# Two orders at the head of the expert stage: the first expert's row splits and the third tile's sum

## The reference, cut to what matters

```python
def moe_ffn(x, ...):
    idx, w = route(xf, w_router, router_bias)          # 8 experts of 64 for each token
    y = routed_experts(...) + swiglu(xf, ws_gate, ws_up, ws_down)
# routed_experts, one block of up to 128 tokens at a time:
    y = swiglu(x_pad[tok], w_gate[e], w_up[e], w_down[e]) * wt[:, None]
    acc = acc.at[tok].add(y)
# and around it, in each layer:
    h = layer_norm(DN_ALPHA * h + ffn, ...)
def swiglu(x, wg, wu, wd):
    return (jax.nn.silu(x @ wg) * (x @ wu)) @ wd
```

## Time and profile before

| | us |
|---|---|
| median of three runs | 2134.94 |
| lowest and highest run | 2131.61 to 2135.66 |
| the profiled execution's own time | 2133.7 |
| its span, first to last instruction | 2131.9 |

### The profile page before, as it was taken

One profiled execution on the slowest core, in us unless ns is written; L12 is line 12 of the kernel. 1 busy time (PEld: TensorE's weight loads), 2 busy tenths in 40 slices (PEclk: granted clock), 3 DMA queues, 4 the chain that ended last, 5 costly groups with the idle time before them and its releaser, 6 DMA issues. The chain is left out here.

```text
span 2131.9 us, 33562 instructions
## 1 busy us (share of the span) xinstructions
PE 1988.9 (93%) x9013; PEld 1495.5 (70%) x9013; DVE 1489.1 (70%) x2484; ACT 1301.5 (61%) x2152; POOL 404.3 (19%) x309
## 2 busy tenths in 40 slices
PE   7998898999999999999978999999999999999994
PEld 6886697667777677777746556756767767777772
DVE  3766667568887788877746137567878778788884
ACT  3544473347787778777743224336777777787874
POOL 0000230012222222222213000001222222222221
PEclk9999999899999999999988999999999999999997
DMA  6320214359999999999974110437999999999994
GB/s 194 134 79 1 69 39 175 131 179 376 367 367 355 352 358 376 370 349 363 354 227 156 54 40 1 172 123 281 354 346 368 361 340 354 365 376 369 376 365 146
DMA packets 181033, 541.72 MB, mean 254 GB/s; under 512 B 26432, under 2 KB 57568, under 8 KB 180832
## 3 DMA queue, kind: packets, MB, share of 16 engines
q1 hardware_dynamic: 150688, 460.65, 57.9%
q0 software_dynamic: 25248, 69.25, 12.9%
q10 hardware_dynamic: 5024, 10.91, 1.3%
HBM read 506.75 MB, written 54.10 MB: 263 GB/s over the span
## 5 line engine op out<-in xcount | busy, mean ns | idle before, releaser
L1830 DVE TENSOR_TENSOR gu_l<-ring,gu_h 128x1024 fp32r<-128x1024 f32 x512 | 610.8, 1221 | 86.0 <-ACT gu_h L1694 75.8
L1694 ACT CAST gu_h<-ring 128x1024 fp32r<-128x1024 f32 x512 | 523.7, 1062 | 74.8 <-DMA ring<-in_moe_w_up 56.6
L1609 PE MATMUL bank<-gu_h,xgT_l 128*128 128x512 f32 x1024 | 416.0, 406 | 0.0
L1611 PE MATMUL bank<-gu_h,xgT_h 128*128 128x512 f32 x1024 | 403.4, 394 | 0.0
L1610 PE MATMUL bank<-gu_l,xgT_h 128*128 128x512 f32 x1024 | 402.0, 393 | 0.0
L1958 POOL DMA_INDIRECT xg<-h_rows,list_idx x128 | 149.6, 1169 | 902.0 <-issue 435.9
L1661 PE MATMUL bank<-ring,hmT_f 128*128 128x512 f32 x536 | 273.4, 591 | 0.0
L1701 ACT CAST down_h<-ring 128x1024 fp32r<-128x1024 f32 x128 | 134.1, 1047 | 223.8 <-PE bank L1661 118.8
L1836 DVE TENSOR_TENSOR down_l<-ring,down_h 128x1024 fp32r<-128x1024 f32 x128 | 156.9, 1225 | 106.6 <-ACT down_h L1701 106.1
L1611 PEld LDWEIGHTS bank<-gu_h,xgT_h 128*128 128x128 f32 x1024 | 193.8, 189 | 43.6
L1977 POOL DMA_INDIRECT moe_sum<-y,out_idx x128 | 193.6, 1512 | 161.9 <-issue 153.5
(11 more groups left out here) (386 smaller groups left out, 3019.0 us busy)
## 6 DMA issues: line engine op xcount, KB each, us to landing
ring<-in_moe_w_gate SPq DMA_DIRECT2D x256, 512.0 KB
ring<-in_moe_w_up SPq DMA_DIRECT2D x256, 512.0 KB
ring<-in_moe_w_down SPq DMA_DIRECT2D x256, 512.0 KB
ring<-in_a_w_in SPq DMA_DIRECT2D x32, 512.0 KB
ring<-in_x SPq DMA_DIRECT2D x8, 512.0 KB, 6.3
ring<-in_a_w_out SPq DMA_DIRECT2D x8, 512.0 KB
moe_sum<-y ACTq DMA_DIRECT2D x8, 512.0 KB, 7.1
ring<-moe_sum SPq DMA_DIRECT2D x8, 512.0 KB, 4.8
```

Source lines behind the costliest of these rows:

```text
L1609: nc.tensor.matmul(out, lhsT=xl, rhs=wh, start=k == 0, stop=False)
L1611: last = nc.tensor.matmul(out, lhsT=xh, rhs=wh, start=False, stop=k == KD - 1)
L1694: nc.scalar.copy(gu_h[:, c, :, :], gate_up_cols(gate_slot, c * CH // 2, CH // 2)).then_inc(gu_hi.sem, 1)
L1830: nc.vector.tensor_tensor(gu_l[:, c, :, :], gate_up_cols(gate_slot, c * CH // 2, CH // 2), gu_h[:, c, :, :].bitcast(F32), ALU.subtract).th ...
```

## The change

In ScalarE's list the high parts of expert 0's rows (`act_rows_T(act, 0, 0)`) move ahead of the store of tile 2's sum. In VectorE's list the column copy and the low parts of expert 0's rows (`dve_slot_w`, `dve_rows_T`) move ahead of tile 2's sum. No instruction is added or taken away there, and no wait is changed. The lists of TensorE, GpSimd and SyncE stay. Beside that, the overflow passes count on other semaphores: two names that reused older semaphores get their own, two that had their own reuse older ones in the first layer.

```diff
-                      "gathered": after(t_copied, 2 * TT), "slot_w": ...
+                      "gathered": sem("over_gathered"), "slot_w": ...
...
-                      "result": after(uw_copied, 2 * TT), "added": after(scan_ready, 2 * TT)}
+                      "result": after(uw_copied, 2 * TT), "added": sem("over_added"), "free": after(scan_ready, 2 * TT), "weights": after(t_copied, 2 * TT)}
             else:
...
-            ov["free"], ov["weights"] = sem(f"over_free{layer}"), sem(f"over_weights{layer}")
+                ov["free"], ov["weights"] = sem("over_free"), sem("over_weights")
...
                     act_hm_T(act, 3, 0, True)
                     act_store_sum(act, 1)
+                    act_rows_T(act, 0, 0)
                     act_store_sum(act, 2)
-                    act_rows_T(act, 0, 0)
                     steps(act, act_step)
...
                     dve_hm_T(v, 3, 0, True)
-                    dve_sum(v, 2)
                     dve_slot_w(v, 0, 0)
                     dve_rows_T(v, 0, 0)
+                    dve_sum(v, 2)
                     steps(v, dve_step)
```

More of the change, by code:

```diff
@@ L1998, in moe @@
                 ov = {"own": after(x_done, 2 * TT), "lists": after(p5_ready, 2 * TT), "slots": after(p5_copied, 2 * TT), "index": after(i5_ready, 2 * TT), "column": after(t_ready, 2 * TT),
-                      "gathered": after(t_copied, 2 * TT), "slot_w": after(p6_ready, 2 * TT), "rowsT": after(p6_copied, 2 * TT), "rowsT_copied": after(i6_ready, 2 * TT), "gate_up": after(y_done64, 2 * TT),
+                      "gathered": sem("over_gathered"), "slot_w": after(p6_ready, 2 * TT), "rowsT": after(p6_copied, 2 * TT), "rowsT_copied": after(i6_ready, 2 * TT), "gate_up": after(y_done64, 2 * TT),
                       "silu": after(ktok_ready, 2 * TT), "product": after(k_scaled, 2 * TT), "hmT": after(v_scaled, 2 * TT), "hmT_copied": after(attn_masked, 2 * TT), "down": after(uw_ready, 2 * TT),
-                      "result": after(uw_copied, 2 * TT), "added": after(scan_ready, 2 * TT)}
+                      "result": after(uw_copied, 2 * TT), "added": sem("over_added"), "free": after(scan_ready, 2 * TT), "weights": after(t_copied, 2 * TT)}
             else:
```

## The result

| | before | after |
|---|---|---|
| median of five runs, us | 2135.11 | 2123.82 |
| lowest and highest, us | 2131.61 to 2137.47 | 2121.43 to 2126.14 |
| profiled execution: span, us | 2131.9 | 2119.6 |

The ratio is 0.9950 with an interval of 0.9938 to 0.9961: 10.7 us faster, between 8.3 and 13.2. A second series gave 0.9958 (0.9945 to 0.9972), 9.0 us. Forecast were 8.8 us and 2126.1; the measured median lies 2.3 us under that and inside the range.

The account below looks back on a forecast made before the run. TensorE (93% busy) and the DMA engines both near their limits, the stage released by its head, where rows wait for a store; (4.2 + 1.5) + 3.1 = 8.8 us, 2134.9 - 8.8 = 2126.1, range 2121 to 2132.5.

Parts of the forecast that it names:

- The wait and its cause: Both heads: expert 0's rows wait behind tile 2's sum, which waits for tile 0's store; TensorE waits 4.70 and 3.19 us.
- Heads: First gate and up matmul of expert 0 comes 4.2 us earlier in the first layer, 2.5 in the second.
- step of 1.46 us: First layer's head: time from the high part's start to TensorE's next transpositions, taken as unchanged by the new order.
- Clock: First matmuls behind both heads: with TensorE's wait at 1.1 us the clock holds, saving 1.5 and 1.1 us more.
- What is late next: Tile 2's sum behind the low parts: unmoved in the first layer, 1.5 us later but hidden in the second.
- SyncE's load: Next weight load, at 465.19 before, comes near 459.5, starting the saturated stream 5.7 us earlier in the first layer.
- `dve_list(3)` in the second layer: VectorE's list that releases expert 3's gather, at 1458.32 before, gains 3.1 us and not 3.6.
- In the first layer TensorE waits for no gather: At 465.22 or 474.94 TensorE waits for no gather, so the first layer's 5.7 us count whole.
- The clock's rival: The clock falls in both heads all the same: gain 6.7 us, time 2128.2; chance 27%.
- ScalarE did stand at tile 2's store: Rival: the wait moves to ScalarE before tile 2's store, handing on only 3.4 us, time 2131.5; chance 12%.
- The gathers made no pattern of new waits: Rival: the stage answers with more gather waits, 0.6 us per expert, and ends slower, 2140 with 23 experts; chance 6%.
- The 1.66 us of the earlier trace: An earlier TensorE wait, after which eight transpositions took 1.97 us, half speed; used to bound when the clock falls.

Follow-up runs that it names:

- third buffer: Kernel before with its old orders, but tile 2's sum in a buffer of its own; median 2128.29, ratio 0.9969, 6.6 us.
- ScalarE half: Kernel before with only expert 0's high parts moved ahead of tile 2's store, VectorE as before; median 2130.96, ratio 0.9985, 3.2 us.
- one-layer kernel: Kernel before with the change in one layer only: first layer 2129.06, ratio 0.9971; second layer 2131.72, ratio 0.9990.
- old orders: Kernel before (2135.11), kernel before with the other overflow-pass semaphores only (2135.75, ratio 0.9999), and kernel before once more (2134.66, ratio 0.9998).
- the last run: Changed kernel with tile 2's down product split and its sum and store behind expert 1's row splits, timed once more: 2123.36, ratio 0.9941 against before.

## Why the prediction was right, step by step

- The wait and its cause. Right: the rows stood behind tile 2's sum, the sum behind tile 0's store. Both parts were shown apart (third buffer, ScalarE half).
- Heads, 4.2 and 2.5 us by adding up the old steps in the new order: 4.32 and 2.67. The step of 1.46 us from high part to next transposition measured 448.68 - 447.23 = 1.45.
- Clock, 1.5 and 1.1 us: 1.39 and 0.98. The choice that a wait of 1.1 us doesn't throw it back was right in all six heads that had it (both of the change in both its profiles, and one in each one-layer kernel).
- What is late next. Tile 2's sum was not moved in the first layer (behind the low parts by the 0.19 us of the store) and hidden in the second; SyncE's load came 6.7 us earlier, 0.98 of it the early start, 5.7 as forecast.
- The one term that was mis-sized: `dve_list(3)` in the second layer gained (1458.32 - 1443.41) - (1444.16 - 1432.88) = 3.6 us and not 3.1. Counted from the first transposition, the three low parts of weights ended 0.3 us sooner than my list of VectorE has them (9.8 us for 10.1), and the product and the fourth low part took 1.5 us where I gave them 1.7.
- What the heads gained did not all arrive at expert 3. "In the first layer TensorE waits for no gather" held for the kernel before, but not for the one after: 0.94 us at expert 3's rows. Up to there the change had gained 4.6 and 3.8 us in the first pair of profiles, and 5.7 and 3.0 in the second pair (both kernels again), 8.4 and 8.7 together for the 8.8 of the sum. That the sum lies so close is in part luck: in the first pair its 5.7 for the first layer is 1.1 too high and its 3.1 for the second 0.7 too low.
- Counted by the heads alone, the 8.8 are 9.4 by the first profiles and 9.0 by the means of all profiles with the old orders; the measured gains are 10.7 and 9.0. The median forecast is off by 2.3 us, and that isn't resolved from scatter.
- Two prices were read wrongly without harm to the forecast. The clock's rival, 6.7 us, has the second group of transpositions at full speed; in rows 6 and 8 they are slow, 1.2 us together, so a fallen clock would have left 5.5. And runs of one kernel do not lie 4 us apart but up to 10.1 (2129.93 to 2140.06 in the series of the first experiments); the medians of its series lie within 1.4 us of each other (2134.53 to 2135.94).
- Rivals. The clock did not fall. ScalarE did stand at tile 2's store (2.71 us), but TensorE had no wait from the first gate and up matmul to the rows of expert 3. The gathers made no pattern of new waits, beside the one at expert 3: 4.5 us in seven waits before and 5.2 in nine after in the first stage, 4.7 in six and 4.0 in nine in the second.

## What to carry to other kernels

An in-order queue passes on every wait ahead of it: look at what stands in front of the operation that the busiest engine waits for, and ask whether that operation has a deadline at all. Here a store's landing held the first rows of a 650 us stage, and the sum that waited for it was itself not due for another 4 us. A stall of TensorE of some us has a second price in the slow transpositions and matmuls behind it, here 3.6 of the heads' 9.4 us. What a head gains can be lost at the next operation that some other list releases, here expert 3's gather behind `dve_list(3)`, so follow the gain past the head. For changes of a few us, profile the unchanged kernel more than once before a difference between two stages is explained.

## What was not expected of the hardware

The clock's answer to a wait is no sharp line. TensorE's waits of 0.88, 1.05 and 1.74 us left it at full speed, and so did one of 2.02 before the transposition at 2026.88 in the last run; 2.31 and 3.07 threw it back. The 1.66 us of the earlier trace rows, which threw it back too, were not a wait by themselves, as the prediction took them: TensorE had waited 0.87 us just before, for a product, with 0.44 us of work between. The first line below is that earlier wait. The other two are from the ScalarE half alone and from the last run, each with a wait of 0.35 or 0.37 us and 0.44 us of work just before:

```profile
1070.43 0.44 PE L1621 MATMUL bank<-const,hm 128*128 128x128 f32 x2 [0.87 <-DVE hm L1811]
...
1067.51 1.32 PE L1583 MATMUL bank<-const,xg 128*128 128x128 f32 x8 [1.68 <-DMA xg<-h_rows,list_idx]
...
1064.76 1.09 PE L1583 MATMUL bank<-const,xg 128*128 128x128 f32 x8 [1.70 <-DMA xg<-h_rows,list_idx]
```

They are nearly alike, yet behind the 1.68 us the clock fell (0.56 in 1068 to 1070), and behind the 1.70 it stayed at 1.00. That the clock held at 1.1 us in six heads of six is shown; how near it came to falling is not.

One program also differs from execution to execution, in a stage's length by 2.5 to 3.4 us and in the start of the first head by 1.2, and whole runs of the kernel before lie up to 10.1 us apart.
